# Moving a tick's second dense group ahead of the transposes in the middle stage of a hybrid decoder step

## The reference

```
h  = RMSNorm(x) * (1 + a1) + s1
[q | k | v | hc | B | C | ga | gb] = h @ w_in
A: stick-breaking attention, 8 heads x 64: beta = sigmoid(q.k/sqrt(d) + b_h),
   A[t,s] = beta[t,s] * prod_{s<j<t}(1 - beta[t,j]), strictly causal; samples also see 2048 cached keys
B: y = B * dwconv3_causal(C * hc)
mix = (sigmoid(ga) * (o_att @ w_att_out) + sigmoid(gb) * (y_conv @ w_conv_out)) @ w_o
x  = x + g1 * mix
x  = x + g2 * sqrelu_mlp(RMSNorm(x) * (1 + a2) + s2)
(s1, a1, g1, s2, a2, g2) = silu(c) @ w_ada + b_ada
```

## Time and profile before

| | |
|---|---|
| median of 3 runs | 1640.53 us (1640.4 to 1642.11) |
| profiled execution, its own time | 1641.08 us |
| its span on the core | 1639.3 us |
| PE busy | 1609.8 us, 98% of the span, 12312 matmuls |
| DVE, ACT, POOL busy | 915.4, 462.9, 607.6 us |
| DMA | 194.74 MB, mean 119 GB/s |

### The profile page before, as it was taken

How to read it: one execution, slowest core, us unless ns; L and a number is a source line. 1 busy time by engine, 2 the same in 40 slices (tenths; PEclk the granted TensorE clock), 3 DMA queues, 4 the chain that set the end, 5 groups by cost and what they waited for, 6 DMA issues and landing times.

```text
span 1639.3 us, 31806 instructions
## 1 busy us (share of the span) xinstructions
PE 1609.8 (98%) x12312; PEld 1501.3 (92%) x12312; DVE 915.4 (56%) x1629; ACT 462.9 (28%) x816; POOL 607.6 (37%) x424
## 2 busy tenths in 40 slices
PE   6999999999999999999999999999999999999999
PEld 5998788878888888889999999999999999999999
DVE  5654364464444345325542699566666666666666
ACT  5444222222222222233222443222222222222220
POOL 0245043243344334322212117444444444444440
PEclk9999999999999999999999999999999999999999
DMA  9113346665656666634332111111111111111112
GB/s 384 47 41 102 130 158 232 232 207 207 196 170 239 229 209 225 208 131 172 120 130 65 39 39 40 52 41 39 51 52 52 52 52 52 53 52 53 52 39 107
DMA packets 72229, 194.74 MB, mean 119 GB/s; under 512 B 8049, under 2 KB 8562, under 8 KB 72082
## 3 DMA queue, kind: packets, MB, share of 16 engines
q1 hardware_dynamic: 67682, 178.62, 31.9%
q10 hardware_dynamic: 4400, 14.10, 2.4%
HBM read 174.26 MB, written 18.42 MB: 118 GB/s over the span
## 4 chain that ended last, share of the span: by engine, by line
PE 92%; DVE 3%; ACT 2%; issue 1%; DMA 1%; POOL 0%; SPq 0%; ACTq 0%; POOLq 0%; DVEq 0%
PE psum L816 78%; PE psum L943 2%; PE psum L966 2%; PE psum L990 2%; PE psum L954 2%; PE psum L1015 2%; PE psum L848 1%; DMA pre<-in_weights 1%; DVE h2L L1827 1%; DVE sc L1859 1%; DVE act L1577 1%; PE psum L868 0%; PE psum L974 0%; PE psum L870 0%; PE psum L869 0%
## 5 line engine op out<-in xcount | busy, mean ns | idle before, releaser
L799 POOL TENSOR_TENSOR wl<-raw,wh 128x512 fp32r<-128x512 f32 x148 | 212.6, 1441 | 317.2 <-ACT wh L1423 317.1
L816 PE MATMUL psum<-hH,wh 128*128 128x352 f32 x808 | 269.1, 333 | 0.1
L816 PE MATMUL psum<-hL,wh 128*128 128x352 f32 x808 | 259.9, 322 | 0.0
L816 PE MATMUL psum<-hH,wl 128*128 128x352 f32 x808 | 259.3, 321 | 0.0
L816 PE MATMUL psum<-hidH,wh 128*128 128x352 f32 x768 | 247.4, 322 | 0.0
L816 PE MATMUL psum<-hidH,wl 128*128 128x352 f32 x768 | 247.2, 322 | 0.0
L816 PE MATMUL psum<-hidL,wh 128*128 128x352 f32 x768 | 247.1, 322 | 0.0
L742 POOL TENSOR_TENSOR beta<-beta,kb 128x512 f32<-128x512 f32 (+3 forms) x96 | 122.4, 1295 | 271.3 <-DVE kb L1629 271.3
L717 POOL TENSOR_TENSOR wl<-raw,wh 128x1024 fp32r<-128x1024 f32 x49 | 119.4, 2437 | 207.0 <-ACT wh L1289 206.5
L816 PEld LDWEIGHTS psum<-hH,wh 128*128 128x128 f32 x808 | 151.5, 188 | 31.2 <-issue 30.1
L1946 DVE SCALAR_TENSOR_TENSOR act<-psum,mods,act 128x352 f32<-128x352 f32 x256 | 145.5, 580 | 50.4 <-PE psum L816 50.4
(11 more groups left out here) (250 smaller groups left out, 3256.0 us busy)
## 6 DMA issues: line engine op xcount, KB each, us to landing
raw<-in_weights SPq DMA_DIRECT2D x152, 512.0 KB, 3.6
ring<-in_cache_k SPq DMA_DIRECT2D x128, 256.0 KB, 3.9
ring<-in_cache_v SPq DMA_DIRECT2D x128, 256.0 KB, 3.5
pre<-in_weights SPq DMA_DIRECT2D x16, 512.0 KB, 16.1
gate_scratch<-gt ACTq DMA_DIRECT2D x14, 528.0 KB, 3.3
act<-gate_scratch SPq DMA_DIRECT2D x14, 528.0 KB, 4.5
xt<-in_xT SPq DMA_DIRECT2D x8, 528.0 KB, 6.8
act<-in_xT SPq DMA_DIRECT2D x8, 528.0 KB, 4.7
```

What stands on the lines that cost most here:

```text
L799: pool.tensor_tensor(xl, source_of(i), x.bitcast(F32), ALU.subtract).then_inc(S["split"], 1)
L816: mm = pe.matmul(out, x, y, start=n == 0, stop=n == end)
```

## The change

Group B moves within a tick: on PE to directly behind group A, ahead of the sample transpose, the prompt's transposes, the modulation's turn and the item scores; on ACT its eviction and `split_high` to directly behind A's, ahead of the AT copy and the item's sigmoid. `SLOTS` gets the same order, which moves B's places in `load_order()` ahead of the item scores' places of the same tick. The lists of DVE and POOL keep their order. Which groups, items and modulation units a tick holds stays as it is.

```
-SLOTS = ("scores", "dense_a", "sturn", "turn", "sscore", "dense_b", "ada", "sav", "av")
+SLOTS = ("scores", "dense_a", "dense_b", "sturn", "turn", "sscore", "ada", "sav", "av")
@@ PE
                 if k in DENSE_A:
                     dense(DENSE_A[k], hH, hL)
+                if k in DENSE_B:
+                    dense(DENSE_B[k], hH, hL)
                 if k in TURN_AT:
                     sample_turn(TURN_AT[k], k)
@@ PE
                 if k in ITEM_AT:
                     sample_scores(ITEM_AT[k], k)
-                if k in DENSE_B:
-                    dense(DENSE_B[k], hH, hL)
@@ ACT
                 if k in DENSE_A:
                     evict(DENSE_A[k], k)
                     split_high(DENSE_A[k])
+                if k in DENSE_B:
+                    evict(DENSE_B[k], k)
+                    split_high(DENSE_B[k])
                 if 0 < k <= NSTEP:
                     turned(k - 1)
                 if k in ITEM_AT:
                     sample_probability(ITEM_AT[k])
-                if k in DENSE_B:
-                    evict(DENSE_B[k], k)
-                    split_high(DENSE_B[k])
```

## The result

| | before | after |
|---|---|---|
| median | 1640.49 us, 4 runs (1640.4 to 1642.11) | 1673.09 us, 4 runs (1667.35 to 1674.01) |
| profiled execution, its own time and span | 1641.08, 1639.3 us | 1673.53, 1671.7 us |
| mean granted clock of the profiled execution | 0.998 | 0.989 |

The medians are 32.6 us apart. Their ratio is 1.0188, with a 95% interval of 1.0175 to 1.0201, which is 29 to 33 us. The forecast was 1655 us with a range to 1663. The sign was right and the size was not: outside the range.

A forecast was written before the change was run, and what follows sets the result against it. TensorE's nearly hole-free list was taken as the bound, with 92% of the chain. Transitions -9.2, lost cover +3.6, VectorE's convolution +9.3 and page loads +10.4 sum to +14.1 us on 1641.1: 1655 us, range 1645 to 1663.

The forecast's parts named there:

- Part 1: TensorE in ticks with an item and a B: cheaper transitions, two stalls gone in ticks 0 and 14; gain 9.2 us.
- Part 2: Eight ticks with a B and no item: values wait for AT copies without B as cover; loss 3.6 us, ends 1 and 7.
- Part 3: VectorE's work behind the item's scan ends 4.1 us later, stalling TensorE around ticks 9, 14 and 20; loss 9.3 us.
- Part 4: Load queue: page loads behind B's raw load stall sample values in ticks 5, 18, 29, 42; 4 x 2.6 = 10.4 us.
- rival (b): Long stalls also lower TensorE's clock, costing 4.7 to 10 us more: 1660 to 1665 us; chance 0.14.
- the deduction of 1.4 us: Page loads of Part 4: one 512 KB raw tile fewer ahead, at 375 GB/s, taking 11.1 us to 9.7.
- The upper end of that term: Part 4's stall per event if nothing is taken off for the raw tile: 4.0 us, against 2.6 forecast.
- Rival (a): Load queue: page loads come in time after all, so Part 4's loss drops out: 1645 us; chance 0.13.
- (c): Stalls of Parts 3 and 4 stay under 5.6 us, so the transitions decide: 1635.5 us, faster; chance 0.08.
- (d): Whole kernel: gains and stalls cancel near 1641 us, needing stalls of 4 to 7 us; chance 0.05.

The follow-up runs named there:

- experiment 1: Load list alone put back (old SLOTS) in the changed kernel, engine orders staying changed: 1652.71 us, ratio 1.0064 to the kernel before.
- Experiment 4: Changed kernel plus 123 filler matmuls with unused results, put in front of the seven long waits: 1662.09 us, ratio 1.0122 to the kernel before.
- experiment 2: Changed kernel with VectorE's order alone adapted: group A's convolution ahead of the transpose copies, modulation copy ahead of B's eviction: 1658.67 us, ratio 1.01.
- experiment 5: Kernel before with the new order of the slots alone, both engines keeping their old order: 1659.91 us, ratio 1.0107.
- experiment 6: Changed kernel with GpSimd's split of B put ahead of its sample product: 1661.15 us, ratio 1.0117 to the kernel before.
- experiment 3: Changed kernel with slots put back and VectorE's order adapted, TensorE's and ScalarE's order as changed: 1640.34 us, ratio 0.9989 to the kernel before.
- experiment 7: B directly behind A only in ticks with an item, except 9 and 20; old slots, modulation copy ahead of B's eviction: 1633.43 us, ratio 0.9951.

## Why the prediction was wrong in size

By its own steps, with the changed kernel's ticks measured from one scores block to the next and held against the same ticks before:

| step | forecast | measured |
|---|---|---|
| Part 1, ticks with an item and a B, ticks 0 and 14 included | -9.2 | -9.2 |
| Part 2, eight ticks without an item | +3.6 | +3.6 |
| Part 3, VectorE's convolution | +9.3 | +9.1 (7.3 - 0.9 that was there before + 2.7) |
| Part 4, page loads | +10.4 | +13.6 |
| clock behind the stalls | 0, a rival | +15.3, the remainder to the span's 32.4 |

In Part 2, ticks 19 and 43 are taken from experiment 1, where no slow matmuls disturb them.

**The step that failed** is the price of a stall in Parts 3 and 4: the sum sets it at the length of the wait, and the clock behind it at nothing. The lower clock stood as rival (b), with a chance of 0.14 and 4.7 to 10 us. It cost 15.3 us by the table's remainder, more than either group of waits (9.1 and 13.6), so that rival was right in kind and too low in size. The granted clock of the changed kernel behind the waits of ticks 5, 10, 15, 18, 21, 29 and 42 (columns as in the earlier trace rows):
```profile
258.80:262.20 3.40, 3.40 (x26) 1.76 (x20) 0.00 (x0) 0.00 (x0) 0.00 (x0) 0.50 0.94 316
310.00:316.80 6.80, 6.17 (x21) 6.21 (x22) 2.69 (x7) 0.00 (x0) 1.71 (x2) 0.50 0.75 254
371.40:378.20 6.80, 6.80 (x20) 5.72 (x21) 2.30 (x4) 0.58 (x1) 2.59 (x2) 0.50 0.62 228
419.20:422.60 3.40, 3.40 (x19) 2.21 (x16) 0.74 (x4) 0.63 (x2) 0.00 (x0) 0.50 1.01 367
449.90:453.30 3.40, 3.40 (x11) 2.70 (x10) 1.98 (x3) 0.58 (x1) 0.66 (x1) 0.50 1.04 404
550.00:556.00 6.00, 5.50 (x43) 3.76 (x44) 1.45 (x3) 1.27 (x2) 0.00 (x0) 1.00 1.03 333
695.70:702.50 6.80, 5.95 (x28) 3.76 (x29) 1.52 (x5) 0.63 (x2) 0.83 (x2) 0.50 0.94 329
```
In the six stretches at 0.50 PE is busy for 29.1 us; at full clock that work would take half as long, so they cost some 14.6 us (an estimate from these rows). Three more measurements bear it. Experiment 4 took 11 us back by matmuls that do nothing. The mean granted clock fell from 0.998 to 0.989, and 0.009 of 1671.7 us is 15.0 us. And among the four runs of the changed kernel the fastest, 1667.35 us, had a clock of 0.993, the others 0.989 and 0.990. The argument against the rival, that dense work on either side protects a single stall, is what the runs refute. The Trainium skill, TensorE: Matmul & The Clock Gate, section HAM oscillation, has the rule that an engine left idle between bursts falls back to 1.2 GHz; the trace agrees, with 0.29 us between matmuls in ticks 15 and 21, but not behind every wait: tick 29's 3.2 us is followed by full clock.

**Part 4 was mis-sized by 0.8 us an event.** The first page issue came 4.2 us into the tick (forecast 4.85), but the deduction of 1.4 us for the raw tile that no longer goes ahead was wrong: from the first page issue to the start of the sample values 258.48 - 252.18 = 6.3 us passed, the full 6.25 of the row (6.2 to 7.0 in the four ticks). The upper end of that term, 4.0 without the deduction, holds the longest wait of the changed kernel, but not those of experiments 2 and 5 (4.6 and 5.5). The fit that the prediction took from the Trainium skill, DMA: Bandwidth & Descriptors, section Anatomy of one DMA, gives 4.4 us for 1 MB and was further off. The page states it for one DMA on GpSimd's path; these are four loads on SP's queue, issued 0.5 us apart behind another tile.

**What was right.** The cause lay in VectorE's and GpSimd's lists, which the diff leaves alone, and in the load list, which the slots reorder, as experiments 1, 2, 5 and 6 show each by itself and experiment 3 for two of them together: the places are those forecast (ticks 5, 18, 29, 42; 10, 15, 21), and the modulation copy ended 4.0 us into tick 21, as worked out from 426.64 + 4.1 against 426.80. The transitions are worth what the rows gave, and with nothing late they show in the time (experiment 7). Rival (a) fell, since the loads were late; (c) and (d) needed stalls under 7 us, and there were 22.7. Part 2 came out right in sum; its eight ticks lie between 0.15 and 0.73 us. Left open: the 1.9 us in experiment 3, and which waits lower the clock and which do not.

## What to carry to other kernels

A move on one engine is a move on every queue whose order is computed from it, or that waits for it: list for each engine what stands behind the moved work's consumers, and subtract its slack at the end of the loop's turn. The load list was the dearest item here, by a single word in a tuple. On a TensorE that is busy throughout, count a stall of some 3 us at more than its length (here 38 us for 22.7 us of waits), and where one can't be avoided, filler matmuls in it give most of the surplus back (11 of 15 us here). A reordering is worth having only in the turns where its price is zero: with the old slots and VectorE's copy ahead, the move in 31 ticks gave -0.1% (experiment 3, which also has VectorE's convolution earlier), and in 21 chosen ticks -0.5% (experiment 7), against +2% for the change as it was made.

## What the runs showed that was not expected

The surplus is uneven. Of the four page waits of the changed kernel, that of tick 29 was followed by matmuls at full pace (the tick is 3.4 us longer than before), those of ticks 5, 18 and 42 by slow ones (5.0, 4.4 and 5.5 us, and ticks 19 and 43 are another 0.8 and 1.3 us longer than in experiment 1). Even the 2.7 us wait of tick 10 lengthened the tick by 5.5. Nor does it take a long wait. In experiment 6 the scores of tick 9 wait 0.83 us for ScalarE, and the clock falls behind them, which makes the tick 2.9 us longer than before the change:
```profile
294.90:298.20 3.30, 3.30 (x13) 3.30 (x12) 2.08 (x3) 1.77 (x3) 1.62 (x2) 0.50 0.81 237
```
In experiment 1 the clock is 0.50 in tick 23 (465.7 to 468.9 us) with no wait since one of 0.81 us at 463.2, a wait that the kernel before has too (448.33 us), at full clock. So the length of the last wait alone does not decide. The time of a kernel with such stalls also scatters: 6.7 us between the lowest and the highest of four runs, against 1.7 for the kernel before.
